# Two chunks' inverses in flight in a delta-rule recurrence, and projections moved off the border between attention heads, in a two-layer hybrid backbone

## The reference

```
# differential attention, 4 heads, two key maps of width 64, values of width 128
q, k, v = split(h @ w_da);  q = rope(rms_norm(q) * gq);  k = rope(rms_norm(k) * gk)
a = softmax(q0 k0') - lam * softmax(q1 k1')
o = rms_norm(a @ v) * (1 - lam_init)

# RWKV-7, 8 heads of width 64, forward and backward
for t in tokens:
    S = S * w_t - (S kk_t) kka_t' + v_t kt_t'
    y_t = S r_t
y = group_norm(y) + bonus;  out = y * gate
```

## Time and profile before

| | |
|---|---|
| median of 3 runs | 4537.6 us (4534.05 to 4546.19) |
| profiled execution | 4534.05 us |
| its span in the trace | 4531.9 us |
| attention stage, each layer | 273 us (352 to 625) |
| recurrence, first inverse to last output, each layer | 566.4 us (709.4 to 1275.8) |
| granted TensorE clock, mean of the execution | 0.93 |

### The profile page before, as it was taken

How to read it: one execution, slowest core, us unless ns; L and a number is a source line. 1 busy time by engine, 2 the same in 40 slices (tenths; PEclk the granted TensorE clock), 3 DMA queues, 4 the chain that set the end, 5 groups by cost and what they waited for, 6 DMA issues and landing times. The chain is left out here.

```text
span 4531.9 us, 81404 instructions
## 1 busy us (share of the span) xinstructions
PE 3915.0 (86%) x34256; PEld 2607.9 (58%) x34256; DVE 1662.6 (37%) x3896; ACT 971.0 (21%) x2266; POOL 223.7 (5%) x226
## 2 busy tenths in 40 slices
PE   5886779999879978999968777799998799699998
PEld 3674446777778843444346644467777787334443
DVE  1445535555532232111124545455555322311111
ACT  2221223333321110000022212233333211100000
POOL 0001100000000000111100011000000000011110
PEclk8998889999989978999979989799999899799999
DMA  5400000000022137999853010000000221389997
GB/s 209 175 6 34 17 31 19 19 17 3 3 100 71 68 162 272 399 393 397 313 211 139 4 34 32 18 17 19 18 3 3 105 70 63 162 309 394 394 398 301
DMA packets 86965, 612.23 MB, mean 135 GB/s; under 512 B 14132, under 2 KB 26420, under 8 KB 52292
## 3 DMA queue, kind: packets, MB, share of 16 engines
q1 hardware_dynamic: 74308, 583.88, 32.8%
q0 software_dynamic: 12288, 23.07, 2.3%
HBM read 581.19 MB, written 30.97 MB: 135 GB/s over the span
## 5 line engine op out<-in xcount | busy, mean ns | idle before, releaser
L2510 PE MATMUL ps<-expert_w,expert_xT 128*64 128x512 f32 x2048 | 459.0, 601 | 3.2 <-DVE expert_xT L2599 3.2
L2510 PEld LDWEIGHTS ps<-expert_w,expert_xT 128*64 128x64 f32 x2048 | 142.6, 138 | 289.0 <-issue 285.3
L1269 PE MATMUL ps<-merge_h_high,merge_w_high 128*128 128x320 f32 x768 | 261.1, 340 | 19.6 <-DVE merge_h_low L1333 19.6
L973 PE MATMUL ps<-w_da,hT 128*128 128x384 f32 x640 | 236.2, 520 | 40.8 <-DVE da_stat L1114 30.7
L1270 PE MATMUL ps<-merge_h_low,merge_w_high 128*128 128x320 f32 x768 | 238.9, 311 | 0.0
L1271 PE MATMUL ps<-merge_h_high,merge_w_low 128*128 128x320 f32 x768 | 238.7, 311 | 0.0
L2515 PE MATMUL ps<-expert_w,expert_xT 128*32 128x256 f32 x4096 | 234.3, 380 | 0.0
L2510 PE MATMUL ps<-expert_w,expert_hT_l 128*64 128x512 f32 x1024 | 226.8, 595 | 0.5 <-ACT expert_hT_l L2584 0.5
L1276 PE MATMUL ps<-yT,merge_w 128*128 128x320 f32 x768 | 222.1, 432 | 0.0
L1587 PE MATMUL ps<-hT,w_rw 128*128 128x320 f32 x640 | 212.2, 459 | 0.6
L2515 PEld LDWEIGHTS ps<-expert_w,expert_xT 128*32 128x32 f32 x4096 | 126.5, 110 | 129.0 <-issue 52.1
(11 more groups left out here) (424 smaller groups left out, 7108.4 us busy)
## 6 DMA issues: line engine op xcount, KB each, us to landing
expert_w<-in_w_expert SPq DMA_DIRECT2D x192, 2048.0 KB, 18.2
w_mod_ring<-in_w_mod SPq DMA_DIRECT2D x32, 1024.0 KB, 7.3
merge_w<-in_w_merge SPq DMA_DIRECT2D x48, 512.0 KB, 3.7
w_mod_first<-in_w_mod SPq DMA_DIRECT2D x8, 2048.0 KB, 14.6
w_ml<-in_w_ml SPq DMA_DIRECT2D x6, 2048.0 KB, 7.8
w_da<-in_w_da SPq DMA_DIRECT2D x8, 1536.0 KB, 6.6
w_rw<-in_w_rw SPq DMA_DIRECT2D x8, 1536.0 KB, 6.4
merge_w<-in_w_merge SPq DMA_DIRECT2D x48, 256.0 KB, 3.9
```

Source lines behind the costliest of these rows:

```text
L973: m = nc.tensor.matmul(g.ps[:, bank_of(h, t), 0:3 * P], g.hT[:, k, tile(t)], w[:, k, :], start=k == 0, stop=k == KB - 1)
L1269: nc.tensor.matmul(bank, high[:, k], xh, start=q == 0 and k == 0, stop=False)
L2510: m = mm(g.ps[64 * n:64 * n + 64, bank, :], lhs, w[:, j, kk, 512 * n:512 * n + 512], start=first, stop=last)
```

## The change

In the recurrence the loop of each engine runs M + 2 times. Iteration c starts the inverse of chunk c (up to its first level), finishes that of chunk c - 1 (levels 1 and 2, half-way, edges), and runs `solve`, `increment` and `output` of chunk c - 2. The products of the two inverses go to banks 0 and 1 in turn, and the masks of the later levels to bank 7, so one bank (6) and one pair of semaphores is left for all side results. `token_major` and `corners` move into banks 3 and 4, behind `mask_b`. Buffers get a third or fourth copy. The identity product L1723 goes: the third power is built as (I + L)(I + L²), with two small additions on DVE (`second`) in place of it. The inverse root of the group norm moves from ACT (with a reciprocal on DVE) to POOL. The running sums of chunk c + 2 instead of c + 1 are made at the end of an iteration. The side work gets new gaps.

In attention the five projections of the next head run in steps 0 to 3 (two of them in step 0), and step 4 holds `turn(h + 1)` and the first scores of the next head. ACT copies queries and keys as well as values out of bank 7. The gains are multiplied into the cosine and sine tables once per layer. The finished head is summed in step 0 of the next and turned back in its step 1, where `finish` stands ahead of `combine`.

```diff
@@ attention: PE @@
                     if h + 1 < H:
-                        project(h + 1, t, 0)
-                    if h and t == 0:
+                        if t == 0:
+                            project(h + 1, 0, 0)
+                            project(h + 1, 0, 1)
+                        elif t + 1 < NT:
+                            project(h + 1, t + 1, 0)
+                        else:
+                            turn(h + 1)
+                    if h and t == 1:
                         turn_back(h - 1)
                     pe.wait_ge(st.comb_ready, T + 1)
...
                     if h + 1 < H:
-                        project(h + 1, t, 1)
+                        if t == 0:
+                            project(h + 1, 1, 0)
+                            project(h + 1, 1, 1)
+                        elif t + 1 < NT:
+                            project(h + 1, t + 1, 1)
+                        else:
+                            scores(T + 1)
...
-                    if t == NT - 1 and h + 1 < H:
-                        turn(h + 1)
-                        scores(T + 1)
@@ attention: ACT, values(h, t) @@
-                    lane(s.copy(val[:, h % 2, t], g.ps[:, bank_of(h, t), 2 * P:3 * P]), st.v_ready)
+                    lane(s.copy(val[:, h % 2, t], g.ps[:, bank_of(h, t), 2 * P:3 * P]), wait=False)
+                    lane(s.copy(qk[:, h % 2, t].rearrange("p m d -> p (m d)"), g.ps[:, bank_of(h, t), 0:2 * P]), st.v_ready)
@@ attention: DVE @@
                 for T in range(H * NT):
                     h, t = T // NT, T % NT
+                    if h and t == 1:
+                        finish(h - 1)
+                    if h + 1 < H and t + 1 == NT:
+                        rotated(h + 1, t)
                     combine(T)
+                    if h + 1 < H and t + 1 == NT:
+                        take_keys(h + 1)
+                    if t + 1 < NT or h + 1 < H:
+                        maxima(T + 1)
                     if h and t == 0:
-                        finish(h - 1)
...
+                        value_sums(h - 1)
+                    if h + 1 < H and t == 0:
+                        token_sums(h + 1, 0)
+                        token_sums(h + 1, 1)
+                    elif h + 1 < H and t + 1 < NT:
+                        token_sums(h + 1, t + 1)
+                    if h and t == 0:
+                        value_scale(h - 1)
+                    if h + 1 < H and t + 1 < NT:
+                        rotated(h + 1, t)
@@ recurrence: one side bank @@
                 def side(h, i):
                     if before(h, i):
-                        pe.wait_ge(side_taken[i % 2], before(h, i))
-                    return g.ps[:, 7 * (i % 2), :]
+                        pe.wait_ge(st.side_taken, before(h, i))
+                    return g.ps[:, 6, :]
@@ recurrence: no identity product @@
                     m.then_inc(st.sq2_ready, 1)
-                    pe.wait_ge(st.first_ready, c + 1)
-                    if c:
-                        pe.wait_ge(st.x_taken, XT * c)
-                    mm(g.ps[:, 1, :], g.c["ident"], flat(first[:]), start=True, stop=False)
@@ recurrence: DVE @@
+                def second(c):
+                    dve.wait_ge(st.sq2_taken, c + 1)
+                    for d in range(2):
+                        lane(v.tensor_tensor(low2[:, :, d], near2[:, :, 1 - d, d], g.c["eye"].unsqueeze(1).to_broadcast([P, 2, RN]), ALU.add),
+                             st.low2_ready if d else None, wait=d)
```

More of the change, by code:

```diff
@@ L1629, in beside, with turn_back @@
+                def turn_back(h, i):
+                    pe.wait_ge(st.yn_ready, h + 1)
+                    bank = side(h + 1, i)
+                    for n, t in enumerate(range(1, NT) if i == EP else (0,)):
+                        m = nc.tensor.transpose(bank[:, tile(n)], y[:, h % 2, t], g.c["ident"])
+                    m.then_inc(st.side_ready, 1)
                 def beside(h, n, gap):
+                    if h >= H:
+                        return
                     more = h + 1 < H
@@ new lines, in beside @@
+                    if n == 2:
+                        if gap in (0, 1) and more:
+                            project(h, R + 1, 2 + gap)
+                        if gap == 2 and h:
+                            turn_back(h - 1, EP)
+                        if gap == 5 and h:
+                            turn_back(h - 1, EP + 1)
+                        if gap in (6, 7) and more:
+                            norm_sums(h, NORM + gap - 6)
+                        if gap >= 8 and more:
+                            ups(h, UPA + gap - 8)
@@ L1829, in _ @@
                     pair_a(0, d)
-                token_major(0)
-                corners(0, 0)
                 for d in range(2):
                     pair_b(0, d)
-                corners(0, 1)
-                for c in range(M):
-                    h, n, ahead = c // NC, c % NC, c + 1 < M
-                    start_inverse(c)
-                    if c:
-                        solve(c - 1)
+                token_major(0)
+                for part in range(2):
+                    corners(0, part)
@@ L1840, in _ @@
+                for c in range(M + 2):
+                    h, n, begun, mid, ahead = c // NC, c % NC, c < M, 0 <= c - 1 < M, c + 1 < M
+                    if begun:
+                        start_inverse(c)
                     beside(h, n, 0)
-                    third_power(c)
-                    if c:
-                        increment(c - 1)
+                    if mid:
+                        lower(c - 1, 1)
+                    if c >= 2:
+                        solve(c - 2)
                     beside(h, n, 1)
-                    eighth_power(c)
@@ L1846, in _ @@
-                    if c:
-                        output(c - 1)
+                    if begun:
+                        third_power(c)
                     beside(h, n, 2)
-                    lower(c, 0)
+                    if mid:
+                        update(c - 1, 1)
+                    if c >= 2:
+                        increment(c - 2)
                     beside(h, n, 3)
-                    update(c, 0)
+                    if begun:
+                        eighth_power(c)
+                    beside(h, n, 4)
@@ L2040, in _ @@
                 corners(0)
[L2041 to L2047 removed]
+                for c in range(M + 2):
+                    h, n, begun, mid, ahead = c // NC, c % NC, c < M, 0 <= c - 1 < M, c + 1 < M
+                    if begun:
+                        squares(c)
                     if ahead:
@@ L2356, in _ @@
                         mask_first(c + 1)
-                    beside(h, n, 3)
-                    mask_level(c, 2)
+                    beside(h, n, 6)
                     if ahead:
                         mask_b(c + 1)
-                    beside(h, n, 4)
-                take_state(M - 1)
-                take_output(M - 1)
+                    beside(h, n, 7)
+                    if c + 2 < M:
+                        sums(c + 2)
                 for part in range(3):
                     centre(H - 1, part)
-                finish(H - 1)
+                for part in range(2):
+                    finish(H - 1, part)
 def route(nc, g, l):
```

770 lines of the change are left out of this document (400 added, 370 removed).

## The result

The changed kernel takes 4569.5 us (median of 10 runs, 4555.3 to 4581.1) against 4541.8 for the kernel before on the same chip (10 runs): a ratio of 1.0059, 95% interval 1.0041 to 1.0076. It is slower by 0.6%, where 4388 was forecast. Attention gained 22.4 us a layer; the recurrence with its prologue lost 43.4 in the first layer and 35.3 in the second; nothing else moved by more than 2.

The account below looks back on a forecast made before the run. PE, in use for 86% of the span, was taken as the bound; gains of 42 us a layer in the recurrence and 32 in attention made 84 + 64 = 148, to 4388 us; range 4335 to 4465, the forecast's own 4360 to 4415.

Parts of the forecast that it names:

- Iterations 2 to 14: 13 x 27.5 = 357.5: Recurrence: 13 iterations laden with side work cost 27.5 us each, where a laden chunk took 29.35 before.
- I put 4 us there, 1.3 in the other four of a head: Recurrence: side-bank waits, 4 us in the iteration with norms and four low-rank products, 1.3 in the others, mean 1.8.
- One side bank replaces the waits: Rival, recurrence: laden iterations wait 4.5 us instead of 1.8, 38 a layer, giving 4464 us; chance 0.14.
- the 520.6 of the sum: Recurrence: forecast length per layer to the last output, prologue's extra left out, against 566.4 us before.
- 3 to 4 us: Recurrence's prologue: extra cost of low-rank products, norms and projections in one bank instead of two.
- It comes off whole: Recurrence: removing the identity product saves its full 0.96 us per chunk, 19 us a layer.
- 32 was forecast: Attention: gain of 32 us a layer, 64 in all, with bounds 10 and 40.
- 15.5 forecast: Attention's border: the context step with two projections takes 15.5 us.
- The 1.7 put down for a low clock: Attention's border: some 1.7 us, within the 15.5, for a first projection half at the low clock.
- The border keeps the low clock: Rival, attention: both projections of step 0 stay at low clock, 8 us per border, giving 4420 us; chance 0.06.
- the rule set beside it: Attention's border: transposes do not count as work for raising the clock, so it would still end at 1.2 GHz.
- DVE becomes the path: Rival, recurrence: DVE's side work in laden chunks lies on the path, 114 us a layer, about 4616 us; chance 0.05.

Follow-up runs that it names:

- run 2: Changed kernel plus 16 unneeded identity products of 256 columns in each of a layer's first three heads: 4524.2 us, 0.9972 of before.
- run 7: Changed kernel plus unneeded identity products only right ahead of waits, ten a head: 4495.6 us; with three more per head where nothing waits: 4497.4 us.
- run 8: Changed kernel with only DVE's order changed (bonus copies ahead of the state's copy, last head's first finish behind the factors): 4494.1 us, 0.9899 of before.
- run 9: Changed kernel with only the prologue changed, its 12 side products alternating between two banks: 4547.7 us, 1.0009 of before.
- run 4: Changed kernel with the removed identity product put back into every start of an inverse, result overwritten: 4568.0 us, 1.0075 of before.
- run 10: Changed kernel with run 8's order and seven products a head: 4485.7 us; plus run 9's prologue: 4466.2; without products: 4483.2; then only bonus copies moved: 4477.8.
- run 3: As run 2, but 14 products of 64x64 by 64 columns in place of each dense one: 4538.4 us, 0.999 of before.
- run 5: Changed kernel with the same side work spread over other gaps: 4515.4 us; plus 16 identity products a head: 4536.0; plus lighter ones instead: 4515.3.

## Why the prediction was wrong

*The failed step* is "Iterations 2 to 14: 13 x 27.5 = 357.5". All its durations were taken at clock 1.00, from the earlier trace rows, and nothing asked whether the new waits would let PE keep that clock. Measured: 421.2. By the clock column at most 55 of the 64 over are the low clock, and the rest waits and the like. For the iteration with the norms I had written "I put 4 us there, 1.3 in the other four of a head", 9.2 in sum; the windows show 2.5 us of PE idle in iteration 7, 3.3 in 8 and 0.9 in 4 to 6 together. So the waits were not too small in sum, if 2 us too low in the fourth iteration, where DVE's copies of the bonus products stand behind the state's. Their price was too small: a wait of 1 to 2 us was followed by 7 to 20 us at half speed. The rival "One side bank replaces the waits" looked at the right place, the side products that wait for their one bank, but counted the length of the waits alone (4.5 us in a laden iteration, 38 a layer), and so long they never were. Runs 2, 7 and 8 show it from both sides: more work in the waits, or fewer waits, bring the clock and 45 to 75 us back.

*The rest of the recurrence.* Iterations 0 and 1: 47.3 against 45.7. From 15 to the last output: 126.0 against 117.4; bare iterations 15 and 16 are 19.5 and 20.1 (forecast 20.2), 17 and 18 are 23.6 and 28.5, again at a fallen clock behind the waits of `finish` and the bonus products, which the last head also has and I had left out. At full clock the 594.5 would be at least 528 (594.5 less the 67 estimated above) against the 520.6 of the sum; run 8 comes to 548.3 at 0.96, or 526 in the same way. The frame of the calculation held to some 2%. The prologue was "3 to 4 us" more and is 14.6 more (45.8 against 31.2): ten small products in a row, each waiting 0.7 to 2.0 for the copy of the last, at a clock of 0.50 to 0.61. Two banks take 13 of them off (run 9).

*The identity product.* "It comes off whole" is right at full clock, where run 4 pays 0.8 to 1.2 us an iteration for it, but the 19 us a layer were not gained: put back, the product gives as much clock back as it costs.

*Attention.* 32 was forecast, 22.4 came. The border is right. PE's timeline of the changed kernel, to be read beside the earlier trace rows, has both projections between two PVs, at full clock:

```profile
447.28 2.50 PE L1067 MATMUL ps<-da_v,da_probT 128*128 128x128 f32 x10
...
451.15 5.43 PE L986 MATMUL ps<-w_da,hT 128*128 128x384 f32 x16
...
457.25 5.43 PE L986 MATMUL ps<-w_da,hT 128*128 128x384 f32 x16 [0.56 <-ACT da_qk L1082]
462.52 0.38 PE L1067 MATMUL ps<-da_v,da_probT 128*128 128x128 f32 x2
```

From PV to PV it is 15.2 us, with 15.5 forecast. The 1.7 put down for a low clock did not fall on the projection but on the PV ahead of it (2.50 instead of 1.28 us). Heads 1 and 3 gained 8.7 (64.0 before, 55.3 now) and 10.2 (50.6 and 40.4). The error is head 0: its context step now carries two projections where it had one. 354.1 to 449.9 is 95.8 us against 91.9 for the same part before, where I had counted a gain; 6.5 of the 9.6 are this, most of the rest head 2 (62.2 and 54.8).

*The rivals.* "The border keeps the low clock" is refuted, and so is what I had drawn from the rule set beside it, that the border would end at 1.2 GHz: 449.9 to 463.4 is at 0.99. By the Trainium skill, "TensorE: Matmul & The Clock Gate", Part 4: PE-mode transpose, transposes don't raise the clock. The trace has a low clock from 443.2 to 450.1, behind transposes with waits of 1.4 to 2.3 us among them; it rose after scores and PV and 1 us ahead of the first projection. So the trace doesn't contradict the rule itself, and can't tell transposes from idleness here either. What mattered in the recurrence is described in the Trainium skill, same page, Part 1, "A second HAM failure mode", for another kernel: PE that idles a little between groups of matmuls swings between the two clocks. The windows cut at the clock's changes agree, with 0.50 and 0.99 in turn between 921.1 and 979.1 us. "DVE becomes the path" did not come about as I put it: DVE is busy 36% of the span, and PE waited for none of the level masks from iteration 2 on; but it was DVE's order that made the longest waits.

Over both layers the misses are 85 and 77 in the recurrence with its prologue (42 forecast as gained, 43.4 and 35.3 lost) and 2 x 9.6 in attention, 182 in sum against the 181 between 4388 and 4569.

## What to carry to other kernels

Where an engine has a clock that depends on what it does, a wait on it costs its length and, perhaps, half of the speed of the work that follows. Before trusting a sum of durations read at full clock, list the waits that the new order makes, and see whether they crowd in one place. Compare stages by the clock column beside the busy share. If a stretch is lost to the clock, first look for the in-order neighbour that makes the wait (here mainly two copies moved ahead of a state copy: 75 us in run 8, 70 between runs 9 and 10 with the copies alone); useless products in the wait itself are the second means, and as good here (74 us).

## What was not expected of the hardware

Added work made the changed kernel faster by 31 to 74 us (runs 3, 2 and 7), though in the spread order of run 5 it did not. The falls came right after waits of 1.0 to 1.9 us between groups, and the clock then stayed down through 17.0 us of which PE was busy for 16.85. Yet not every such wait does it: iteration 16 waits 1.1 at `token_major` and stays at full clock. What makes the difference was not settled. Filling products of 64x64 held the clock in iterations 7 and 8 like those of 128x128 (both 1.00).
